# A second DMA queue for every other chunk of expert weights

## The chip, the core and the metric

The kernel runs on one core of a Trainium2 chip. The engines named below are TensorE (PE, matmuls), VectorE (DVE), ScalarE (ACT), GpSimd (POOL) and SyncE (SP), which here only asks for transfers and waits. Transfers from device memory (HBM) into the core's working memory are carried by 16 DMA engines; they are asked for in queues, which the profile numbers (q1 is the queue of SyncE, q10 that of ScalarE, q0 that of GpSimd). The metric is the device time of one execution in microseconds. Three executions of the kernel before took 1761.07, 1762.66 and 1762.74 us, a median of 1762.66.

## The reference

One layer of a diffusion backbone over 384 tokens (128 context tokens, 256 latent ones) of 1024 channels, in float32: a mixer (differential attention beside a two-directional state-space scan), then a mixture of 16 experts in which each expert chooses its tokens. Only the second half matters here:

```
def expert_choice_ffn(h, w_router, w_gate, w_up, w_down):
    xf = h.reshape(ntok, d)
    aff = jax.nn.softmax((xf @ w_router).astype(jnp.float32), axis=-1)
    gates, idx = lax.top_k(aff.T, cap)          # cap = 2 * tokens / 16: 16 context, 32 latent tokens
    xe = xf[idx]
    he = silu(einsum('ecd,edf->ecf', xe, w_gate)) * einsum('ecd,edf->ecf', xe, w_up)
    ye = einsum('ecf,efd->ecd', he, w_down) * gates[..., None]
    out = zeros_like(xf).at[idx.reshape(-1)].add(ye.reshape(-1, d))
```

Each expert has w_gate and w_up of 1024 x 2048 and w_down of 2048 x 1024, 24 MB in float32, so 384 MB for the 16 experts, and each weight is used once.

## The kernel before

The mixer comes first and takes a little under half of the time. The experts' weights are laid out ahead as 12 chunks an expert (`EC`), 192 in all, which I number n = 12 e + c for expert e and chunk c. A chunk is one transfer of 2 MB: 128 partitions, 16 KB each. Chunks c = 0 to 7 are alternately gate and up weights (c even: gate, c odd: up), four pairs j = 0 to 3. Chunks 8 to 11 are the down weights, two for each half of the output.

TensorE takes the chunks strictly in order, 32 matmuls a chunk (line 1002). After a gate and up pair ScalarE computes a Silu of the gate half (line 1483), VectorE multiplies the up half to it (line 2131), and TensorE later turns the product round (line 959) for the down chunks, which start only when the fourth product is turned. After chunks 9 and 11 ScalarE copies the result out (line 1491). After chunks 10 and 11 of every fourth expert TensorE combines the results of the four into the token rows (`combine`, lines 944 and 946). In the first four experts TensorE also has other pieces of work between chunks, lines 902 to 922.

The chunks lie in six slots (`FF_SLOTS`), and each slot has a semaphore of its own that its transfer raises by 16 when it has landed. Chunks 6, 7 and 8 of the first expert lie elsewhere, in early buffers. Chunk n + 6 may be asked for when chunk n has been used, since they share a slot; chunk 15 comes into the slot of chunk 9. What tells that a chunk is used is `ff_used` for an even c, `gu_ready` for c = 1, 3, 5, 7, and `d_ready0` and `d_ready1` for c = 9 and 11.

SyncE asks for all chunks, in the order of their use, in its one queue: `wait_used` waits for the slot, `load` asks (line 1039). Chunks 9 to 23 are written out one by one, the rest stand in a loop over experts 2 to 15. ScalarE, VectorE and TensorE run the experts in four groups of four: the first, a loop of two rounds for the middle two, and the last.

Of the kernel before, what the change touches and what calls it, by code (L numbers as in the profile page):

```python
# [33 lines left out]
NE, CAP_P, CAP_S, D_FF = 16, 16, 32, 2048  # L34
CAP = CAP_P + CAP_S
HALF = P // 2
GE = 4
# [6 lines left out]
FF_SLOTS = 6  # L44
# [34 lines left out]
EC = 12  # L79
# [86 lines left out]
def build(nc, t_in, t_out, consts, scratch):  # L166
    ctx = ExitStack()
    with ctx:
# [4 lines left out]
        def sem(name):  # L173
            if name not in sems:
                sems[name] = ctx.enter_context(nc.semaphore(name))
            return sems[name]

        def at(kib, *shape):

            n = int(np.prod(shape))  # L180
            off = int(kib * 256)
            assert off + n <= 53184, (kib, shape)
            v = arena[:, off:off + n]
            if len(shape) == 1:
                return v
            names = "abcd"[:len(shape)]
            return v.rearrange(f"p ({' '.join(names)}) -> p {' '.join(names)}",
                               **{k: s for k, s in zip(names[1:], shape[1:])})


        slots = [at(16 * s, KT, CW) for s in range(FF_SLOTS)]
# [112 lines left out]
        mixer_w, expert_w, dt_cols = t_in["mixer_chunks"], t_in["expert_chunks"], t_in["dt_columns"]  # L304
# [32 lines left out]
        pieces += [("xe_s", k) for k in range(KT)] + [("xe_p", n) for n in range(KT // 2)] + [("gate", n) for n in range(4)]  # L337
        beside_experts = {(n // 6, n % 6): p for n, p in enumerate(pieces) if p}
        piece_no = {p: n for n, (_, p) in enumerate(sorted(beside_experts.items()))}

        def y_sq(t, half):
            n = {0: 44, 1: 28, 2: 30}[t] + half
            return stat[:, n:n + 1]

        def of_group(g, r, per, add):

            return per * g + add if r is None else r * per + (per + add)
# [674 lines left out]
        @block.sync  # L1022
        def _(sp):
            sp.dma_start(vecs, t_in["vectors"]).then_inc(sem("vec_in"), 16)
            sp.dma_start(x_cm.rearrange("p k n -> p (k n)"), t_in["x_cm"]).then_inc(sem("x_in"), 16)
            def used(*key):
                name, value = AT["chunk_end"][chunk_no[key]]
                sp.wait_ge(sem(name), value)

            for n in range(NM - 2):  # L1030
                slot, m = chunk_slot[n], last_in_slot[n]
                if slot in (2, 3) and m is None:
                    sp.wait_ge(sem("ssd_over"), 1)
                if m is not None:
                    name, value = AT["chunk_end"][m]
                    sp.wait_ge(sem(name), value)
                sp.dma_start(weight_slot[slot].rearrange("p k n -> p (k n)"), mixer_w[n]).then_inc(sem(f"w_in_slot{slot}"), 16)
            def load(e, c, s):
                sp.dma_start(slots[s].rearrange("p k n -> p (k n)"), expert_w[e, c]).then_inc(sem(f"ff_slot{s}"), 16)

            def load_early(c, dst, k0):
                n_ = dst.shape[1]
                sp.dma_start(dst.rearrange("p k n -> p (k n)"), expert_w[0, c, :, k0 * CW:(k0 + n_) * CW])\
                  .then_inc(sem(f"ff_early{c}"), 16)

            def wait_used(e, c):

                if c >= 8 and c % 2:
                    sp.wait_ge(sem(f"d_ready{(c - 8) // 2}"), e + 1)
                elif c % 2:  # L1050
                    sp.wait_ge(sem("gu_ready"), e * 4 + (c // 2 + 1))
                else:
                    sp.wait_ge(sem("ff_used"), e * 6 + (c // 2 + 1))

            used("ga", 1)
            load(0, 0, 2)
            used("ada", 9)
            load(0, 1, 3)
            sp.wait_ge(sem("attn_over"), 1)
            for n in (NM - 2, NM - 1):  # L1060
                slot = chunk_slot[n]
                sp.dma_start(weight_slot[slot].rearrange("p k n -> p (k n)"), mixer_w[n]).then_inc(sem(f"w_in_slot{slot}"), 16)
            load(0, 3, 5)
            used("out", 0)
            load(0, 4, 0)
            used("out", 1)
            load(0, 5, 1)
            load_early(7, early_7a, 0)
            load_early(7, early_7b, 6)
            used("ada", 10)  # L1070
            load_early(6, early_6, 0)
            sp.wait_ge(sem("yg_ready"), 6)
            load_early(8, early_8a, 0)
            used("ada", 11)
            load(0, 2, 4)
            sp.wait_ge(sem("x_free"), AT["routed"])
            load_early(8, early_8b, 4)
            for n in range(9, 24):
                m = n - 9 if n < 15 else n - 6
                wait_used(m // 12, m % 12)  # L1080
                load(n // 12, n % 12, (n + 5) % FF_SLOTS)
            with sp.Fori(2, NE) as e:
                for c in range(12):
                    wait_used(e - 1 if c < 6 else e, (c - 6) % 12)
                    load(e, c, (c + 5) % FF_SLOTS)
            for n, t in enumerate(TILES):
                sp.wait_ge(sem("out_ready"), n + 1)
                dst = t_out["xs"][0, (t - 1) * P:t * P, :] if t else t_out["xp"][0]
                sp.dma_start(dst, x[:, t, :]).then_inc(sem("x_stored"), 16)
            sp.wait_ge(sem("x_stored"), 16 * NT)  # L1090
# [100 lines left out]
        def _(act):  # L1191
# [266 lines left out]
            def diagonals(n):  # L1458
                if n >= 2:
                    act.wait_ge(sem("piece_ready"), piece_no["gate", n - 2] + 1)  # L1460
                cnd, j = n // 2, n % 2
                for q in range(4):
                    act.activation(diag[:, n % 2, q, :], ident, ACT.Copy,
                                   scale=gpost[:, KT + 4 * j + q, cnd:cnd + 1]).then_inc(sem("diag2_ready"), 1)

            for j in range(2):
                act.activation(route[:, 4 + j:5 + j], stat[:, 32 + j:33 + j], ACT.Copy).then_inc(sem(f"d_free{j}"), 1)

            def group(g, r=None):

                first, final = g == 0, g == NE // GE - 1

                def N(per, add):
                    return of_group(g, r, per, add)

                for i in range(GE):
                    if first and i == 1:
                        diagonals(0)
                        diagonals(1)
                    for j in range(4):  # L1480
                        act.wait_ge(sem("gu_ready"), N(16, 4 * i + j + 1))
                        act.wait_ge(sem("h_done"), N(16, 4 * i + j + 1))
                        act.activation(sg[:, j % 2, :], psum[:, j % 2, 0:2 * P], ACT.Silu).then_inc(sem("sg_ready"), 1)  # L1483
                        if first and i == GE - 1 and j < 2:
                            diagonals(2 + j)
                    for j in range(2):
                        act.wait_ge(sem(f"d_ready{j}"), N(GE, i + 1))
                        for q in range(1 if final and i == GE - 1 and j else 2):
                            c0 = j * CW + q * 2 * P
                            for dst, lo in ((stage_s, 0), (stage_p, CAP_S)):  # L1490
                                cp = act.activation(dst[CAP_S * i:CAP_S * (i + 1), c0:c0 + 2 * P],  # L1491
                                                    psum[HALF * q + lo:HALF * q + lo + CAP_S, 5 + j, 0:2 * P], ACT.Copy)
                        cp.then_inc(sem(f"d_free{j}"), 1)
                        if final and i == GE - 1:
                            for n, t in enumerate(TILES):
                                act.wait_ge(sem("comb_done"), N(6, 3 * j + n + 1))
                                act.activation(last_sq[:, j, t, :], y[:, t, j * CW:(j + 1) * CW], ACT.Square, scale=D ** -0.5,
                                               accum_out=y_sq(t, j)).then_inc(sem("last_sq_ready"), 1)

            group(0)  # L1500
            with act.Fori(0, NE // GE - 2) as r:
                group(None, r)
            group(NE // GE - 1)


        @block.vector
# [706 lines left out]
```

## Time and profile before

| | |
|---|---|
| median of three executions | 1762.66 us |
| the profiled execution | 1757.46 us, of which its span 1755.7 us |
| TensorE busy | 1546.1 us, 88% of the span |
| VectorE / ScalarE busy | 475.7 us / 326.0 us |
| moved by DMA | 512.91 MB, 489.89 MB of it in SyncE's queue |
| DMA rate, second half of the span | 423 to 428 GB/s in each slice but the last |

The page cuts the span in 40 slices of 43.9 us and gives for each the busy share of the engines and of the 16 DMA engines, and the GB/s that they moved. A share of idle time matters only on the path that sets the end; the chain of waits names that path. In the table of DMA issues "to landing" is the time from the instruction that asks to the last byte landed, with what stands ahead of it in the queue. A matmul that is held up by a transfer is listed as waiting for "DMA arena<-in_expert_chunks".

### The profile page before, as it was taken

What the parts mean: (1) busy time and instruction counts of PE and PEld (TensorE: products, weight loads), DVE (VectorE), ACT (ScalarE), POOL (GpSimd) and SP (SyncE); (2) the same over time, 40 slices, a digit from 0 to 9 for tenths busy, and PEclk for the clock granted to TensorE, in tenths of its full rate; (3) what the DMA queues carried; (4) which work ended last, traced back from release to release, by engine and by line L of the source; (5) the groups of instructions that cost most, each with busy time, mean ns of one, the idle gap of its engine ahead of it and who ended that gap; (6) DMA issues with size and microseconds to landing.
All of it is one profiled execution on the core that took longest, in us unless ns stands there. A gap on an engine that the chain in (4) does not pass through costs nothing.

```text
span 1755.7 us, 22492 instructions
## 1 busy us (share of the span) xinstructions
PE 1546.1 (88%) x9269; PEld 917.5 (52%) x9269; DVE 475.7 (27%) x1181; ACT 326.0 (19%) x897; POOL 88.4 (5%) x116
## 2 busy tenths in 40 slices
PE   6999999999999999999999888777888787877776
PEld 4655555565545555556666455444455454544443
DVE  2336778740015555325111110000100000100003
ACT  1327565610012222012100100000000000000001
POOL 0002222200000001000000000000000000000000
PEclk9999999999999999999999999999999999999999
DMA  8234344224331523369999999999999999999995
GB/s 350 96 111 168 120 151 137 91 90 185 126 108 48 192 96 117 125 287 386 372 428 427 428 426 427 428 427 428 426 423 427 426 428 427 428 427 427 428 428 216
DMA packets 40593, 512.91 MB, mean 292 GB/s; under 512 B 4640, under 2 KB 4768, under 8 KB 10544
## 3 DMA queue, kind: packets, MB, share of 16 engines
q1 hardware_dynamic: 34416, 489.89, 67.2%
q0 software_dynamic: 5936, 21.01, 3.5%
q8 instruction: 77, 1.26, 0.3%
q10 hardware_dynamic: 144, 0.59, 0.1%
q14 instruction: 20, 0.16, 0.0%
HBM read 506.65 MB, written 4.82 MB: 291 GB/s over the span
## 4 chain that ended last, share of the span: by engine, by line
PE 55%; DMA 32%; DVE 7%; ACT 4%; issue 2%; SPq 0%; DVEq 0%; POOL 0%; ACTq 0%
DMA arena<-in_expert_chunks 32%; PE psum L1002 17%; PE psum L656 7%; PE psum L411 6%; PE psum L422 5%; PE psum L628 5%; PE psum L712 2%; PE psum L820 2%; PE psum L434 1%; ACT arena L1320 1%; ACT arena L1308 1%; PE psum L463 1%; PE psum L704 1%; DVE arena L1725 1%; PE psum L944 1%
## 5 line engine op out<-in xcount | busy, mean ns | idle before, releaser
L1002 PE MATMUL psum<-arena 128*64 128x256 f32 x6144 | 705.6, 385 | 139.8 <-DMA arena<-in_expert_chunks 107.9
L1002 PEld LDWEIGHTS psum<-arena 128*64 128x64 f32 x6144 | 437.6, 138 | 401.4 <-DMA arena<-in_expert_chunks 152.3
L2131 DVE TENSOR_TENSOR arena<-arena,psum 128x256 f32<-128x256 f32 x64 | 27.0, 421 | 703.3 <-ACT arena L1483 703.3
L411 PE MATMUL psum<-arena 128*128 128x384 f32 x512 | 168.9, 487 | 2.8 <-ACT arena L1227 2.8
L411 PEld LDWEIGHTS psum<-arena 128*128 128x128 f32 x512 | 96.2, 190 | 68.6 <-issue 3.3
L656 PE MATMUL psum<-arena 128*128 128x384 f32 x384 | 129.6, 491 | 0.0
L1483 ACT ACTIVATE arena<-psum 128x256 f32<-128x256 f32 x64 | 24.6, 384 | 564.8 <-PE psum L1002 564.8
L422 PE MATMUL psum<-arena 128*128 128x512 f32 x288 | 127.9, 600 | 0.0
L1491 ACT ACTIVATE arena<-psum 32x256 f32<-32x256 f32 x126 | 47.3, 375 | 274.5 <-PE psum L1002 273.4
L656 PEld LDWEIGHTS psum<-arena 128*128 128x128 f32 x384 | 72.5, 193 | 46.9 <-issue 3.2
L1105 POOL TENSOR_TENSOR arena<-arena 128x1 f32<-128x1 f32 x45 | 25.9, 577 | 1332.0 <-DVE arena L2172 941.6
L422 PEld LDWEIGHTS psum<-arena 128*128 128x128 f32 x288 | 55.7, 195 | 68.7 <-issue 67.9
L628 PE MATMUL psum<-arena 128*128 128x384 f32 x256 | 83.3, 487 | 1.8 <-DVE arena L1702 1.2
L628 PEld LDWEIGHTS psum<-arena 128*128 128x128 f32 x256 | 48.5, 190 | 36.3 <-DVE arena L1702 1.5
L1308 ACT ACTIVATE arena<-arena 128x128 f32<-128x128 f32 x192 | 57.2, 386 | 0.0
L712 PE MATMUL psum<-arena 128*128 128x384 f32 x128 | 42.1, 487 | 2.1 <-DVE arena L1849 1.7
L820 PE MATMUL psum<-arena 128*128 128x512 f32 x96 | 42.5, 595 | 0.0
L959 PE MATMUL psum<-arena 128*128 128x128 f32 x128 | 27.5, 297 | 13.0 <-DVE arena L2097 12.9
L463 PE MATMUL psum<-arena 128*128 128x128 f32 (+1 forms) x215 | 36.3, 279 | 1.7 <-DVE arena L1940 1.7
L1384 ACT ACTIVATE arena<-psum,arena 128x384 f32<-128x384 f32 (+1 forms) x48 | 24.0, 506 | 65.4 <-DVE arena L1827 65.4
L463 PEld LDWEIGHTS psum<-arena 128*128 128x128 f32 (+1 forms) x215 | 25.3, 140 | 20.2 <-issue 14.6
L712 PEld LDWEIGHTS psum<-arena 128*128 128x128 f32 x128 | 24.1, 190 | 19.2 <-issue 2.4
(274 smaller groups left out, 1130.4 us busy)
## 6 DMA issues: line engine op xcount, KB each, us to landing
arena<-in_expert_chunks SPq DMA_DIRECT2D x190, 2048.0 KB, 25.4
arena<-in_mixer_chunks SPq DMA_DIRECT2D x40, 2048.0 KB, 8.5
arena<-cs_rows POOLq DMA_DIRECT2D x24, 512.0 KB, 5.1
arena<-in_h_cm POOLq DMA_DIRECT2D x8, 256.0 KB, 3.2
out_state<-arena POOLq DMA_DIRECT2D x8, 256.0 KB, 2.6
arena<-in_expert_chunks SPq DMA_DIRECT2D x2, 1024.0 KB, 15.9
arena<-in_x_cm SPq DMA_DIRECT2D x1, 1536.0 KB, 8.7
arena<-in_expert_chunks SPq DMA_DIRECT2D x1, 1536.0 KB, 11.1
```

Source lines behind the costliest of these rows:

```text
L411: mm = pe.matmul(b[:, 0:NTOK], w[:, k, ct * P:(ct + 1) * P], src[:, k, :], start=k == 0, stop=k == KT - 1)
L422: mm = pe.matmul(b[:, :], h1T[:, k, t * P:(t + 1) * P], w[:, k, :], start=k == 0, stop=k == KT - 1)
L463: mm = pe.transpose(b[0:width, at_:at_ + rows], src, ident[0:rows, 0:rows])
L628: mm = pe.matmul(psum[:, (n0 + ct) % 4, 0:NTOK], w[:, k, ct * P:(ct + 1) * P], oT[:, k2 * KT + k, :], start=k2 == 0 and k == 0, stop=k2 == ...
L656: mm = pe.matmul(b[:, 0:NTOK], w[:, k, n % 4 * P:(n % 4 + 1) * P], h1T[:, k, :], start=k == 0, stop=k == KT - 1)
L712: mm = pe.matmul(psum[:, o_bank[ct], 0:NTOK], w[:, k, ct % 4 * P:(ct % 4 + 1) * P], oTa[:, k, :], start=k == 0, stop=k == KT - 1)
L820: mm = pe.matmul(b[:, :], mergedT[:, k, t * P:(t + 1) * P], w_o[:, k, :], start=k == 0, stop=k == KT - 1)
L959: mm = pe.transpose(psum[:, 4, a * P:(a + 1) * P], h_sb[:, j % 2, a * P:(a + 1) * P], ident)
L1002: mm = pe.matmul(psum[HALF * q:HALF * (q + 1), bank, 0:2 * P], src[:, k0 + k, :], w_k[:, 2 * P * q:2 * P * (q + 1)], start=bool(opens and ...
L1308: last = act.activation(e_, e_, ACT.Identity, scale=-1.0, bias=cs[:, t, 32 * d + 8 * g + h:32 * d + 8 * g + h + 1])
L1491: cp = act.activation(dst[CAP_S * i:CAP_S * (i + 1), c0:c0 + 2 * P], psum[HALF * q + lo:HALF * q + lo + CAP_S, 5 + j, 0:2 * P], ACT.Copy)
L2131: dve.tensor_tensor(h_sb[:, j % 2, :], sg[:, j % 2, :], psum[:, 2 + j % 2, 0:2 * P], ALU.mult)\
```

## The change

From chunk 15, the sixteenth, on, SyncE asks only for chunks of even number. ScalarE asks for those of odd number, in its own queue: for chunk n + 6 right after its wait for the gate and up pair that ends in chunk n (before the Silu), or right after its wait for the down half that ends in chunk n (before the copies). Slots, semaphores and the condition for each chunk are as before. The loop of ScalarE over the two middle groups is written out, since the chunk numbers are now needed while the program is built.

```
             for n in range(9, 24):
                 m = n - 9 if n < 15 else n - 6
-                wait_used(m // 12, m % 12)
-                load(n // 12, n % 12, (n + 5) % FF_SLOTS)
+                if m < 6 or n % 2 == 0:
+                    wait_used(m // 12, m % 12)
+                    load(n // 12, n % 12, (n + 5) % FF_SLOTS)
             with sp.Fori(2, NE) as e:
-                for c in range(12):
+                for c in range(0, 12, 2):
                     wait_used(e - 1 if c < 6 else e, (c - 6) % 12)
                     load(e, c, (c + 5) % FF_SLOTS)
...
+            def load_six_on(e, c):
+
+                n = EC * e + c + FF_SLOTS
+                if 15 <= n < NE * EC:
+                    sl = (n + 5) % FF_SLOTS
+                    act.dma_start(slots[sl].rearrange("p k n -> p (k n)"), expert_w[n // EC, n % EC])\
+                       .then_inc(sem(f"ff_slot{sl}"), 16)
+
...
                     for j in range(4):
                         act.wait_ge(sem("gu_ready"), N(16, 4 * i + j + 1))
+                        load_six_on(GE * g + i, 2 * j + 1)
                         act.wait_ge(sem("h_done"), N(16, 4 * i + j + 1))
...
                     for j in range(2):
                         act.wait_ge(sem(f"d_ready{j}"), N(GE, i + 1))
+                        load_six_on(GE * g + i, 9 + 2 * j)
...
-            group(0)
-            with act.Fori(0, NE // GE - 2) as r:
-                group(None, r)
-            group(NE // GE - 1)
+            for g in range(NE // GE):
+                group(g)
```

SyncE's loop over experts 2 to 15, its first half, before. A row is an instruction with what it waits for; the DMA rows each ask for one chunk, the rows between compute the number to wait for.

```order
L1039 ISA [waits ff_used]
L1039 DMA arena<-in_expert_chunks 128x4096
L1051 ISA
L1039 ISA [waits gu_ready]
L1039 DMA arena<-in_expert_chunks 128x4096
L1053 REGISTER_ALU
L1039 ISA [waits ff_used]
L1039 DMA arena<-in_expert_chunks 128x4096
L1039 ISA [waits d_ready0]
L1039 DMA arena<-in_expert_chunks 128x4096
```

The same place in SyncE's loop after the change.

```order
L1039 ISA [waits ff_used]
L1039 DMA arena<-in_expert_chunks 128x4096
L1053 REGISTER_ALU
L1039 ISA [waits ff_used]
L1039 DMA arena<-in_expert_chunks 128x4096
L1053 REGISTER_ALU
```

Of four chunks asked for in one queue two are left, and both wait for `ff_used`; the ones behind `gu_ready` and `d_ready0` are gone from it.

ScalarE in the first expert, from its last Silu on, and the start of the second expert, before. Line 1483 is the Silu, line 1491 the copies of a down half, line 1463 a piece of other work.

```order
L1483 ACTIVATE arena<-psum 128x256 [waits h_done,gu_ready] x3
L1491 ACTIVATE arena<-psum 32x256 [waits d_ready0]
L1491 ACTIVATE arena<-psum 32x256 x3
L1491 ACTIVATE arena<-psum 32x256 [waits d_ready1]
L1491 ACTIVATE arena<-psum 32x256 x3
L1463 ACTIVATE arena<-arena 128x128 x8
L1483 ACTIVATE arena<-psum 128x256 [waits h_done,gu_ready] x4
```

The same place after. Line 1472 asks for a chunk; the Silu is now line 1493, the copies line 1502, the other work line 1464.

```order
L1493 ACTIVATE arena<-psum 128x256 [waits h_done,gu_ready] x3
L1472 DMA arena<-in_expert_chunks 128x4096 [waits d_ready0]
L1502 ACTIVATE arena<-psum 32x256 x4
L1472 DMA arena<-in_expert_chunks 128x4096 [waits d_ready1]
L1502 ACTIVATE arena<-psum 32x256 x4
L1464 ACTIVATE arena<-arena 128x128 x8
L1472 DMA arena<-in_expert_chunks 128x4096 [waits gu_ready]
L1493 ACTIVATE arena<-psum 128x256 [waits h_done]
```

The first transfer that moves to ScalarE is chunk 15, behind `d_ready0` of the first expert; from then on each of the six waits of an expert has one behind it, ahead of the arithmetic.

## Rows read from the trace of the kernel before

**Rows 1.** The page: DMA busy tenths and GB/s in 40 equal slices.

```profile
DMA  8234344224331523369999999999999999999995
GB/s 350 96 111 168 120 151 137 91 90 185 126 108 48 192 96 117 125 287 386 372 428 427 428 426 427 428 427 428 426 423 427 426 428 427 428 427 427 428 428 216
```

**Rows 2.** Stretches: length, busy us (x instructions) by engine, PEclk, DMA share, GB/s.

```profile
855.00:857.00 2.00, 2.00 (x20) 1.22 (x16) 0.00 (x0) 0.34 (x1) 0.00 (x0) 1.00 0.00 0
...
870.00:1700.00 830.00, 682.48 (x5662) 415.00 (x5658) 72.10 (x171) 66.46 (x177) 0.00 (x0) 0.99 1.01 427
...
1285.00:1295.00 10.00, 10.00 (x91) 6.35 (x89) 0.53 (x2) 0.77 (x2) 0.00 (x0) 1.00 0.99 411
```

**Rows 3.** Waits, 870 to 1735 us: us in total, times, longest.

```profile
PEld psum L1002 <- DMA arena<-in_expert_chunks: 152.3, 105, 2.8
```

**Rows 4.** The chain that ended last: start us, us, what.

```profile
1616.88 25.48 DMA arena<-in_expert_chunks
1646.25 25.48 DMA arena<-in_expert_chunks
```

**Rows 5.** TensorE's last four chunks: start us, us, line [idle before <- releaser].

```profile
1719.85 0.20 PEld L959 LDWEIGHTS psum<-arena 128*128 128x128 f32 x2 [0.38 <-issue]
...
1722.21 3.67 PE L1002 MATMUL psum<-arena 128*64 128x256 f32 x32 [0.52 <-DVE arena L2097]
...
1731.98 3.67 PE L1002 MATMUL psum<-arena 128*64 128x256 f32 x32 [1.04 <-DMA arena<-in_expert_chunks]
1735.59 0.30 PEld L944 LDWEIGHTS psum<-arena 128*128 128x128 f32 x2 [0.39 <-issue]
...
1738.36 3.67 PE L1002 MATMUL psum<-arena 128*64 128x256 f32 x32
```

**Rows 6.** Stretches while the last chunks land.

```profile
1725.00:1726.00 1.00, 0.89 (x10) 0.29 (x5) 0.00 (x0) 0.00 (x0) 0.00 (x0) 1.00 1.03 426
1726.00:1727.00 1.00, 0.00 (x0) 0.00 (x0) 0.00 (x0) 0.00 (x0) 0.00 (x0) 1.00 0.57 229
...
1732.00:1734.00 2.00, 2.00 (x20) 1.35 (x22) 0.00 (x0) 0.51 (x2) 0.00 (x0) 1.00 0.50 213
...
1736.00:1738.00 2.00, 2.00 (x6) 0.76 (x4) 1.08 (x2) 0.53 (x1) 0.00 (x0) 1.00 0.00 0
```

**Rows 7.** DMA queues, stretch 2 to 5 us: packets, MB, share.

```profile
q10 hardware_dynamic: 144, 0.59, 49.2%
q1 hardware_dynamic: 146, 0.41, 36.9%
```

**Rows 8.** TensorE, ScalarE and SyncE around chunks 10 to 15, and TensorE one expert later.

```profile
856.66 48.19 SPq L1039 DMA_DIRECT2D arena<-in_expert_chunks  x12
856.66 1.54 ACT L1491 ACTIVATE arena<-psum 32x256 f32<-32x256 f32 x4 [9.03 <-PE psum L1002]
...
864.78 7.13 PE L1002 MATMUL psum<-arena 128*64 128x256 f32 x64
...
873.32 7.13 PE L1002 MATMUL psum<-arena 128*64 128x256 f32 x64
```

**Rows 9.** What asking costs: duration ns min/median/max; then issue to landing.

```profile
L1039 SPq DMA_DIRECT2D arena<-in_expert_chunks x189: 327/333/462, 748.9 to 1710.3; - x189
...
DMA to landing us min/median/max: 7.5/25.4/28.8
```

**Rows 10.** The one DMA that ScalarE asks for, by its line.

```profile
L1210 ACTq DMA_DIRECT2D arena<-shape_consts x1: 412/412/412, 0.7 to 0.7; - x1
```

**Rows 11.** TensorE where its loop over the middle groups turns back.

```profile
1262.52 3.67 PE L1002 MATMUL psum<-arena 128*64 128x256 f32 x32
...
1269.65 1.02 PE L946 MATMUL psum<-arena 128*128 128x512 f32 x2
1274.40 0.86 PE L1002 MATMUL psum<-arena 128*64 128x256 f32 x5 [3.73 <-issue]
1279.53 14.91 PE L1002 MATMUL psum<-arena 128*64 128x256 f32 x123 [4.27 <-issue]
```

## The prediction

> **What bounds the kernel now.** I read the page's slices first. From slice 21 to slice 39 the DMA engines are busy all the time and the rate hardly moves, 423 to 428 GB/s [rows 1]. The stretch 870 to 1700 us says the same in one row: 427 GB/s at a share of 1.01, with TensorE busy 682 of 830 us [rows 2]. Then the waits: in the experts TensorE's weight loads are held up 105 times by expert chunks, 152.3 us in all [rows 3]. Last the chain of waits: near the end it is one transfer after another, 25.48 us each, and the pieces stand 1646.25 - 1616.88 = 29.37 us apart for six chunks, 4.895 us a chunk [rows 4], against 3.67 us of matmuls [rows 5]. So from about 865 us on the end is: the time at which the last byte has landed, plus what TensorE still has to do then. The change can move three things: the rate, the order in which chunks land, and idle time of the DMA engines.
>
> **How the last chunks run.** The last expert's chunk 10 (n = 190) starts at 1731.98, held up by its transfer; chunk 11 (n = 191) starts at 1738.36, and not for want of data: it follows the combine, 1738.36 - 1735.59 = 2.8 us [rows 5]. By the pace chunk 191 lands at 1731.94 + 4.9 = 1736.8; the DMA engines are at rest from 1736 on [rows 6]. I call the landing of the last byte T and take 1736 to 1736.8. Behind the start of chunk 191 nothing depends on a transfer, so the end moves as that start moves. The last chunk thus has about 2 us of slack today, and chunk 190 has none.
>
> **Part 1: the asking moves.** 89 chunks (n = 15, 17, ..., 191) go from SyncE to ScalarE. An issue takes SyncE 0.333 us [rows 9]; the only one of ScalarE took 0.412 us [rows 10]. So ScalarE gets 89 x 0.33 to 0.41 = 30 to 37 us more work, in front of Silus and copies, in a stretch of 900 us where it is busy 66 of 830 us [rows 2]. Behind the issue on ScalarE's queue stand the Silu, then VectorE's product, then TensorE's turn; but only the fourth Silu of an expert is waited for at once, and there the gap between the third turn and chunk 8 is 1722.21 - 1719.85 = 2.4 us [rows 5] and would grow by 0.33 to 0.41. What hides this is the DMA-bound pace: TensorE has 4.9 - 3.7 = 1.2 us of room a chunk. In the last expert, where the gap could count, its fourth wait has no chunk behind it (n would be 193). Cost 0; with the cover gone 15 x 0.33 to 15 x 0.41 = 5 to 6 us. SyncE loses the same issues and half its register work; it is not on the path: gain 0. Is ScalarE late for a slot? The slots of odd chunks come free exactly at its own waits, and it had idled 9.03 us when chunk 9 was used, at 856.66, the same moment at which SyncE asked for chunk 15 [rows 8]. Cost 0, at most some tenths of a microsecond at the one place where it matters: the DMA engines are at rest at 855 to 857 us and wait for this issue [rows 2]. Below zero there is nothing to gain, since the slot isn't free earlier.
>
> The written out loop: ScalarE's program is longer and doesn't turn back. TensorE and VectorE still do. Where TensorE turns back it stands idle 3.73 and 4.27 us [rows 11], and no slot comes free between the end of a chunk at 1262.52 + 3.67 = 1266.2 and that of the next, some 3 us after 1279.53 [rows 11]; six slots cover it nearly, the rate falls to 411 GB/s for 10 us [rows 2], worth 0.4 us. No effect of the change there as long as some four chunks stay queued. Value 0, bounds -1 and +3 (the upper one if only three chunks, 14.7 us, are queued there, as in the second rival below).
>
> **Part 2: two queues share the engines.** Before, chunk n has all 16 engines and n + 1 stands behind it. After, both are under way at once. Does the trace show sharing? Only once: at 2 to 5 us ScalarE's queue has 144 packets served and SyncE's 146, both with work left [rows 7]. Packet for packet, equal turns. A chunk is 128 equal rows of 16 KB whatever its number, so each queue gets half: a chunk takes 9.8 us instead of 4.9, and two are under way. No data are lost: T stays if the rate stays, since about five chunks are asked for at any time (25.4 us to landing [rows 9]) and neither queue runs dry.
>
> What changes is the order at the end. When chunk 190 lands, part of 191 is left, which then runs at full rate. If 191 follows at a distance d in the shared pace, 190 lands d/2 before T, where it landed 4.9 us before. The distance is set when the queues fill, at 865 to 900 us: TensorE frees the slot of an even chunk 3.57 us before that of the odd one (7.13 / 2), and the next even one 8.54 - 3.57 = 4.97 us later [rows 8]. So the queues start almost in alternation, d between 3.6 and 4.9, and as turns are equal it stays. I take 4.3: chunk 190 lands 2.15 us before T, at 1733.9 to 1734.7 instead of 1731.94: 2.0 to 2.7 us later, I take 2.3. The rest follows unchanged: 3.67, combine, chunk 191, the tail. Bounds of the tail without drift: d = 4.9 gives +1.6 (T = 1736), and both landing together (d = 0) gives +4.9.
>
> In the Trainium skill, "DMA: Bandwidth & Descriptors", section "Queues, rings and completion order", each DMA engine takes turns between queues packet by packet; the row above agrees. By that rule alone the sum is +2.3. The section "Issuing engines are not separate DMA queues" says that issuing from a second engine saves only the time to ask; by it there is no gain in rate here, which no row shows or excludes.
>
> **Part 3: the rate.** No row shows two queues with long transfers over a long time, so I bound it. Upward: at 1726 the rate falls from 426 to 229 GB/s, and stays near 213 until 1734 [rows 6]: half of the engines were done 8 us before the other half. Each engine has the same bytes, so the slow half is 8 of 870 us, 0.9%, slower. If two queues brought it to the pace of the fast half, T would come 8 us earlier. Downward: the worst stretch of 10 us in the rows has 411 GB/s [rows 2]; that over 870 us would be 870 x (427/411 - 1) = 34 us, but there it was missing slots. The row nearest to the case is the long one, 427 GB/s, with hardly any variation, and I take 0, with ends -8 and +34, of which I hold more than +8 (1%) unlikely.
>
> **Sum.** 0 + 0 + 2.3 + 0 = +2.3 us. The profiled execution took 1757.46 us (span 1755.7), so 1759.8 for it. The median of the timed ones is 5.2 us above the profiled one; I carry the difference over: 1762.66 + 2.3 = 1765.0 us.
>
> **Rivals.**
> A: two queues fill gaps between transfers. For: the slow half of the engines has 0.9% to gain. Against: share 1.01 in the long stretch leaves no gap to see. Then -8 + 2.3 = -5.7: 1757.0 us.
> In the same page of the Trainium skill, section "Where 436 GB/s comes from", the ceiling is 435 GB/s; by it the most to gain would be 1.9% of 870 us, some 16 us, an estimate from that page.
> B, the slower side: turns aren't equal, or the distance drifts, and one queue runs ahead until the slots stop it. It decides as soon as one queue gets 1% more: 4 us more in 400 us. Then the late queue has the engines alone at the end, one chunk per 4.9 us, each followed by one that has long landed. If the odd queue is ahead, 188 lands at T - 4.9, about 1731.9, and 188, 189 and 190 follow, 11.0 us, then 2.8 of combining: 191 starts at 1745.7 instead of 1738.36, +7.4. If the even queue is ahead, 187 lands at about 1727.0; four chunks 14.7, the gap 2.4, combining 2.8: 1746.9, +8.5. For: half the engines are already 0.9% off the other half. Against: the equal packets of rows 7. 1770 to 1771 us.
> C: alternating between queues costs rate, 1% or more. For: nothing in the trace. Against: the 427 GB/s don't suffer from the small packets of other queues. +8.7 + 2.3 = +11: 1773.7 us.
> D: ScalarE's issues aren't hidden, or an issue stalls its engine while the queues are full. Against: SyncE's issues take 0.333 us with five chunks queued, at most 0.462 [rows 9]. +5 to +6 on top: 1771 us.
>
> **Chances.** Forecast 0.43 (own range +0.5 to +5, 1763 to 1768); A 0.2; B 0.2; C 0.1; D 0.07. What a measurement can tell from no change is 0.2%, 3.5 us. Faster: A, 0.2. Same: about four fifths of the forecast's case and a little of A's, 0.37. Slower: the rest of the forecast's case, B, C and D, 0.43. The range takes in A and B and leaves out half of C: 1756 to 1772.
>
> **What would show it.** Queue q10 with 89 transfers of 2 MB and q1 with the others; to-landing times near 25 us in both. A rate of 427 GB/s in the middle, else A or C. Landings alternate with some 4 and 5 us between them: TensorE's waits for data then stay single; if it waits before every second chunk only, for twice as long, that is B. The last two chunks within 2 to 3 us of each other, chunk 190 starting 2 to 3 us later against T. A gap before chunk 8 that is 0.3 to 0.4 us longer, without effect. Wrong it would be if the long stretch's rate is off by over 0.3%, or if chunk 190 starts at the old distance from T.

## The result

The change made the kernel slower by little: the ratio to before is 1.0023, with a 95% interval of 1.0015 to 1.0032, or about 4 us (2.6 to 5.6). The medians of 20 executions each are 1763.95 us (1760.9 to 1768.4) after and 1761.05 us (1757.7 to 1763.8) before, 2.9 us apart. The forecast was 1765.0 us, which is +2.3 on a base of 1762.66 from three executions.

The profiled execution of after has a span of 1761.7 us, 6.0 more than that of before. The page's slices and its table of queues:

```profile
DMA  8234334224321423279999999999999999999994
GB/s 349 96 110 167 120 135 152 94 86 190 120 107 49 191 96 136 105 292 401 374 428 427 427 426 427 427 427 427 427 384 427 427 427 427 426 428 427 427 427 202
```

```profile
arena<-in_expert_chunks SPq DMA_DIRECT2D x101, 2048.0 KB, 25.0
arena<-in_expert_chunks ACTq DMA_DIRECT2D x89, 2048.0 KB, 25.6
```

Against [rows 1] the rate is the same to 2 GB/s from the 21st slice on, but for the last one, in which the transfers end (202 for 216), and one near 1290 us: 384 where 423 stood. The two queues split the chunks as meant, and their times to landing are those of [rows 9]. Three stretches of after (length, busy us by engine, PEclk, DMA share, GB/s):

```profile
870.00:1700.00 830.00, 690.23 (x5630) 420.91 (x5626) 71.81 (x171) 66.33 (x177) 0.00 (x0) 0.97 1.00 425
1285.00:1295.00 10.00, 10.00 (x74) 6.03 (x72) 0.37 (x1) 0.38 (x1) 0.00 (x0) 0.77 0.66 242
1738.00:1739.00 1.00, 1.00 (x8) 0.55 (x6) 0.00 (x0) 0.00 (x0) 0.00 (x0) 0.50 0.00 0
```

In the long stretch of [rows 2] 2 GB/s are missing, and the second row has them: for 10 us the rate is 242 GB/s, 43% under the 427 of elsewhere, where before had 411 GB/s. The third row is chunk 190: TensorE's granted clock is 0.50, its lower level of 1.2 GHz. TensorE's last chunks in after, to be held against [rows 5] (start us, us, line, what ended the idle time before):

```profile
1724.03 0.44 PE L959 MATMUL psum<-arena 128*128 128x128 f32 x2
...
1726.60 7.30 PE L1002 MATMUL psum<-arena 128*64 128x256 f32 x64 [0.72 <-DVE arena L2106]
...
1736.30 5.36 PE L1002 MATMUL psum<-arena 128*64 128x256 f32 x32 [2.41 <-DMA arena<-in_expert_chunks]
1741.59 1.98 PE L944 MATMUL psum<-arena 128*128 128x512 f32 x4
...
1743.41 1.02 PE L946 MATMUL psum<-arena 128*128 128x512 f32 x2
...
1744.37 3.67 PE L1002 MATMUL psum<-arena 128*64 128x256 f32 x32
```

And the DMA engines while the last bytes land, against [rows 6]:

```profile
1736.50:1737.00 0.50, 0.50 (x6) 0.34 (x4) 0.00 (x0) 0.00 (x0) 0.00 (x0) 0.76 0.39 164
1737.00:1737.50 0.50, 0.50 (x6) 0.30 (x4) 0.00 (x0) 0.00 (x0) 0.00 (x0) 0.50 0.08 33
```

I read from these rates that the last byte is moved at about 1737.3, and chunk 190 starts 1.0 us ahead of that. Before, it started 3.9 us ahead (1731.98 against about 1735.9). That is 2.9 us, the order of landing. Chunk 190 then takes 5.36 us instead of 3.67: 1.7 us. And the last byte itself comes later.

The rows of the last two requests say the same more sharply, since the time of asking and the time to landing add up to the landing. First chunk 190, asked for by SyncE, then chunk 191, asked for by ScalarE:

```profile
L1039 SPq DMA_DIRECT2D arena<-in_expert_chunks x1: 333/333/333, 1710.8 to 1710.8; - x1
DMA to landing us min/median/max: 25.4/25.4/25.4
...
L1472 ACTq DMA_DIRECT2D arena<-in_expert_chunks x1: 335/335/335, 1714.4 to 1714.4; - x1
DMA to landing us min/median/max: 23.7/23.7/23.7
```

Chunk 190 lands at 1736.3 (the chain of waits has it as 1710.82 + 25.44), when TensorE starts on it, and chunk 191 at 1738.1, 1.8 us behind. In before the same two rows give 1705.3 + 26.7 = 1732.0 and 1710.3 + 26.5 = 1736.8, one chunk's 4.9 us apart. So the order of landing is worth about 3 us. A landing is reported about 1 us after the rate has gone to zero, in before as in after.

To compare single executions I count from the start of the experts' first chunk, since what comes ahead of it varies by up to 5 us from one execution to the next, in kernels that are the same up to there. That chunk starts at 816.49 in before and 816.97 in after:

```profile
816.49 7.13 PE L1002 MATMUL psum<-arena 128*64 128x256 f32 x64 [0.92 <-DVE arena L2045]
```

```profile
816.97 7.13 PE L1002 MATMUL psum<-arena 128*64 128x256 f32 x64 [0.92 <-DVE arena L2054]
```

From there to the start of chunk 191 it is 921.9 us before and 927.4 after, +5.5 us. The sum: the last byte 919.4 to 920.3 us after the start, +0.9; the order +2.9; the clock +1.7. Behind the start of chunk 191 both kernels are alike (17.3 us to the end of the span). The 5.5 us of this pair of profiles lie at the upper end of what the executions give, 2.6 to 5.6 us by the ratio; the section on the prediction comes back to that.

### The profile page after: what moved, and what is told of

The parts are those of the page before. It is cut to its first block, busy times and chain, and to the rows that moved or that the text cites. A ratio compares the mean times of both kernels' runs of the same rounds, so it can differ in the third digit from the quotient of the medians.

```text
span 1761.7 us, 22164 instructions
## 1 busy us (share of the span) xinstructions
PE 1559.6 (89%) x9269; PEld 926.8 (53%) x9269; DVE 478.2 (27%) x1181; ACT 325.8 (18%) x897; POOL 88.0 (5%) x116
## 4 chain that ended last, share of the span: by engine, by line
PE 54%; DMA 34%; DVE 6%; ACT 3%; issue 2%; ACTq 0%; DVEq 0%; SPq 0%; POOL 0%
DMA arena<-in_expert_chunks 33%; PE psum L1002 16%; PE psum L656 7%; PE psum L411 6%; PE psum L422 6%; PE psum L628 5%; PE psum L712 2%; PE psum L820 2%; PE psum L434 1%; ACT arena L1309 1%; ACT arena L1321 1%; PE psum L944 1%; PE psum L463 1%; PE psum L704 1%; PE psum L610 1%
## 5 line engine op out<-in xcount | busy, mean ns | idle before, releaser
L1002 PE MATMUL psum<-arena 128*64 128x256 f32 x6144 | 716.8, 390 | 126.0 <-DMA arena<-in_expert_chunks 89.3
L1002 PEld LDWEIGHTS psum<-arena 128*64 128x64 f32 x6144 | 446.6, 140 | 390.5 <-DMA arena<-in_expert_chunks 127.8
L411 PEld LDWEIGHTS psum<-arena 128*128 128x128 f32 x512 | 96.2, 190 | 68.6 <-issue 3.3
L656 PEld LDWEIGHTS psum<-arena 128*128 128x128 f32 x384 | 72.5, 193 | 46.9 <-issue 3.2
L422 PEld LDWEIGHTS psum<-arena 128*128 128x128 f32 x288 | 55.9, 195 | 69.1 <-issue 68.3
L628 PEld LDWEIGHTS psum<-arena 128*128 128x128 f32 x256 | 48.5, 190 | 36.3 <-DVE arena L1711 1.5
L959 PEld LDWEIGHTS psum<-arena 128*128 128x128 f32 x128 | 12.9, 140 | 40.8 <-DVE arena L2140 22.4
## 6 DMA issues: line engine op xcount, KB each, us to landing
arena<-in_expert_chunks ACTq DMA_DIRECT2D x89, 2048.0 KB, 25.6
```

The costliest lines, as they stand in the source:

```text
L411: mm = pe.matmul(b[:, 0:NTOK], w[:, k, ct * P:(ct + 1) * P], src[:, k, :], start=k == 0, stop=k == KT - 1)
L422: mm = pe.matmul(b[:, :], h1T[:, k, t * P:(t + 1) * P], w[:, k, :], start=k == 0, stop=k == KT - 1)
L628: mm = pe.matmul(psum[:, (n0 + ct) % 4, 0:NTOK], w[:, k, ct * P:(ct + 1) * P], oT[:, k2 * KT + k, :], start=k2 == 0 and k == 0, stop=k2 == ...
L656: mm = pe.matmul(b[:, 0:NTOK], w[:, k, n % 4 * P:(n % 4 + 1) * P], h1T[:, k, :], start=k == 0, stop=k == KT - 1)
L959: mm = pe.transpose(psum[:, 4, a * P:(a + 1) * P], h_sb[:, j % 2, a * P:(a + 1) * P], ident)
L1002: mm = pe.matmul(psum[HALF * q:HALF * (q + 1), bank, 0:2 * P], src[:, k0 + k, :], w_k[:, 2 * P * q:2 * P * (q + 1)], start=bool(opens and ...
```

## The experiments

The table gives for each kernel the ratio to before with its interval, and from its profile the time from the start of the experts to the last byte (T) and to the start of chunk 191. T is read from the rate, good to half a microsecond only. The last column is how far chunk 190 lands ahead of chunk 191, from the rows of their requests as above, good to 0.1 us.

| kernel | ratio (95%) | to T | to chunk 191 | 190 ahead of 191 |
|---|---|---|---|---|
| before | 1 | 919.4 | 921.9 | 4.9 |
| the change | 1.0023 (1.0015 to 1.0032) | 920.3 | 927.4 | 1.8 |
| e1, only the written out loop | 0.9997 (0.9988 to 1.0006) | 918.8 | 921.7 | 4.9 |
| e2, last expert in one queue | 0.9998 (0.9989 to 1.0007) | 920.2 | 922.6 | 4.9 |
| e3, one queue, last two swapped | 1.0042 (1.0028 to 1.0056) | 919.0 | 927.9 | -4.9 |
| e4, change, TensorE written out | 1.0010 (1.0001 to 1.0019) | 917.5 | 922.7 | 1.8 |
| e5, before, TensorE written out | 0.9992 (0.9981 to 1.0002) | 918.2 | 920.7 | 4.9 |
| e6, e4 with last expert in one queue | 0.9992 (0.9983 to 1.0000) | 917.3 | 919.9 | 4.9 |
| e7, change, long filler | 1.0033 (1.0021 to 1.0045) | 920.6 | 928.2 | 1.6 |
| e8, e5 with chunk 190 in halves | 0.9986 (0.9978 to 0.9995) | 917.5 | 918.6 | 4.8 (its first half 7.3) |
| e9, change, short filler | 1.0021 (1.0012 to 1.0030) | 919.4 | 925.0 | 1.8 |
| e10, change, chunk 191 by SyncE | 1.0004 (0.9996 to 1.0013) | 919.9 | 922.8 | 4.9 |

**e1: the written out loop of ScalarE alone.**

```
-            group(0)
-            with act.Fori(0, NE // GE - 2) as r:
-                group(None, r)
-            group(NE // GE - 1)
+            for g in range(NE // GE):
+                group(g)
```

> Only ScalarE's loop is written out; SyncE asks for every chunk in its one queue, as before. Theory 1 (the order in which the last chunks land costs the time): no change, within 0.1% of before; chunk 190 starts some 4 us ahead of the last byte. Rival (the longer program of ScalarE, or what it fetches, costs the time): +3 us, like the whole change.

Measured 0.9997. The longer program costs nothing that can be seen; the queues are what matters.

**e2: two queues, but the last expert's chunks all by SyncE.**

```
-            with sp.Fori(2, NE) as e:
+            with sp.Fori(2, NE - 1) as e:
...
+            for c in range(12):
+                wait_used(NE - 2 if c < 6 else NE - 1, (c - 6) % 12)
+                load(NE - 1, c, (c + 5) % FF_SLOTS)
...
-                if 15 <= n < NE * EC:
+                if 15 <= n < (NE - 1) * EC:
```

> Two queues as in the change up to chunk 179; the last expert's twelve chunks (180 to 191) are all asked for by SyncE, in order. Theory 1: chunk 190 again lands one chunk's time (4.9 us) before 191, the end comes 3 to 4.5 us earlier than with the change, so equal to before within 0.1%, unless engines were idle in the middle. Rival (the rate, or an idle spell of the DMA engines in the middle, costs the time): nothing is won, still +3 us against before.

Measured 0.9998, the interval (0.9989 to 1.0007) below that of the change. Its profile has the same hole in the transfers as after (246 GB/s from 1285 to 1295 us), and T as late; but chunk 190 starts about 4 us ahead of T, at full clock:

```profile
1733.28 3.67 PE L1002 MATMUL psum<-arena 128*64 128x256 f32 x32 [1.41 <-DMA arena<-in_expert_chunks]
1736.88 1.98 PE L944 MATMUL psum<-arena 128*128 128x512 f32 x4
1738.70 1.02 PE L946 MATMUL psum<-arena 128*128 128x512 f32 x2
1739.65 3.67 PE L1002 MATMUL psum<-arena 128*64 128x256 f32 x32
```

So the loss sits in the last dozen chunks, not in the 83 that ScalarE asks for before.

**e3: the late chunk 190 without a second queue.**

```
+            wait_used(NE - 1, 5)
+            load(NE - 1, 11, (11 + 5) % FF_SLOTS)
+            load(NE - 1, 10, (10 + 5) % FF_SLOTS)
```

(in place of the last two loads in the order 10, 11).

> One queue as before, but SyncE asks for chunk 191 ahead of chunk 190 (it waits for the slot of 191 first). The cost of a late chunk 190 by itself, with no second queue: it lands with the last byte, 4.9 us later against it. Theory 1: +4 to +5 us against before from the order, and +1.7 us more if TensorE's clock falls to half in chunk 190 after the longer wait, so +5 to +7 us (0.3 to 0.4%). Rival (landing order doesn't matter, since chunk 191 has slack): 0 to +2 us.

Measured 1.0042 (+7 us, 5 to 10). The whole 4.9 us of a chunk are paid, and the clock on top (4.99 us instead of 3.67; the granted clock is 0.50 from 1738 to 1741 us):

```profile
1739.55 4.99 PE L1002 MATMUL psum<-arena 128*64 128x256 f32 x32 [6.75 <-DMA arena<-in_expert_chunks]
```

The order of landing costs what it says, in one queue as in two. The rival, that chunk 191's slack covers it, is out.

**e5: TensorE's loop written out, one queue.** The diff is that of e1 with `pe` for `act`.

> One queue as before; TensorE's loop over the two middle groups is written out, so that it doesn't turn back. If turning back alone made TensorE stand still (3.73 and 4.27 us) and the DMA rate dip (411 GB/s at 1285 us), both go, and the time falls by at most 1 us: the dip was worth 0.4 us. If it is program fetch behind the transfers of weights, in whatever form the program has, gaps of the same size stay, and the longer program could add new ones: up to +5 us.

Measured 0.9992, the interval just reaching 1. Where TensorE stood still before [rows 11] it now goes on 1.05 us after the combine. Elsewhere in the experts its longest idle time that no other engine and no transfer accounts for is 2.5 us:

```profile
1274.73 1.02 PE L946 MATMUL psum<-arena 128*128 128x512 f32 x2
1276.80 14.03 PE L1002 MATMUL psum<-arena 128*64 128x256 f32 x128 [1.05 <-DVE arena L2118]
```

So the standing still comes with the turning back; the same instructions, written out, have none of it. What TensorE does in that time no row shows.

**e4: the change, TensorE's loop written out.**

> The change, with TensorE's loop over the middle groups written out. Theory 1 with its second half (the queues keep their distance until an idle spell of the DMA engines resets it; that spell comes from TensorE turning back): no stretch at 242 GB/s near 1290 us, so the last byte lands 1 to 1.4 us earlier against the start of the experts; TensorE waits some 1.2 us before every chunk to the end instead of 2.1 us before every second; chunk 190 lands 2.4 instead of 2.0 us ahead of the last byte. +0.5 to +2.5 us against before. Rival (the distance drifts by itself, turns are unequal): pairs come back, +3 to +5 us as with the change.

Measured 1.0010, inside what theory 1 gave. The hole is gone, and T is 2.8 us earlier, more than the 1 to 1.4 expected. The chunks stay apart to the end: TensorE waits before each one, 0.6 and 1.5 us in turn, where after has 7.34 us of two chunks and then 2.1 us of waiting.

```profile
1285.00:1295.00 10.00, 10.00 (x92) 6.44 (x90) 0.76 (x2) 0.38 (x1) 0.00 (x0) 1.00 1.00 424
```

```profile
1708.51 3.67 PE L1002 MATMUL psum<-arena 128*64 128x256 f32 x32 [0.59 <-DMA arena<-in_expert_chunks]
...
1714.03 3.67 PE L1002 MATMUL psum<-arena 128*64 128x256 f32 x32 [1.48 <-DMA arena<-in_expert_chunks]
...
1733.60 3.67 PE L1002 MATMUL psum<-arena 128*64 128x256 f32 x32 [1.86 <-DMA arena<-in_expert_chunks]
```

A pair in after, for comparison:

```profile
1706.97 7.34 PE L1002 MATMUL psum<-arena 128*64 128x256 f32 x64 [2.07 <-DMA arena<-in_expert_chunks]
```

One part was expected wrongly: chunk 190 does not land 2.4 us ahead of chunk 191 but 1.8, as in after (1708.1 + 25.5 = 1733.6 and 1712.2 + 23.2 = 1735.4), though there was no idle spell. So the idle spell is not what brings the last two together. Against e5, the same kernel with one queue, the order costs about 3 us (4.9 - 1.8), T is 0.7 earlier, and chunk 191 starts 2.0 us later, 0.11%. By the two ratios it is 0.18%; their intervals, 0.1% to either side, hold both.

**e6: both mended.** Two queues to chunk 179, the last expert by SyncE, TensorE written out.

> Two queues up to chunk 179, the last expert by SyncE alone, TensorE's loop written out. It stands to the kernel with one queue and TensorE written out (0.9992 of before) as two queues in the middle stand to one, with neither the idle spell nor the late chunk 190. Theory 1: the same as that kernel, 0.999 of before. Rival (two queues cost or gain rate in the middle): off by 0.2% or more either way; a gain of the slow half of the DMA engines would show as up to 8 us.

Measured 0.9992, the same as e5. Two queues in the middle neither win nor lose, to the 0.15% (2.6 us) that two such intervals can tell apart: this also excludes the 8 us that the slow half of the DMA engines might have won.

**e7: matmuls in front of chunk 190.**

```
+                        if final and i == GE - 1 and c == 10:
+                            for _ in range(5):
+                                pe.matmul(psum[:, 7, :], ident, hT.rearrange("p k s -> p (k s)")[:, 0:CW], start=True, stop=True)
```

> The change, with five matmuls more (some 2.5 us, their result is not used) on TensorE ahead of its wait for chunk 190. If the clock falls in chunk 190 because TensorE stood still ahead of it, chunk 190 takes 3.67 us instead of 5.36 and the end comes 1.7 us earlier, +1 to +2.5 us against before. Rival (the clock falls for what TensorE did over a longer time): no gain, +3 us or a little more.

Measured 1.0033: the filler was mis-sized. It took 4.56 us, not 2.5, and ended when chunk 190 had landed for some time. But chunk 190 itself ran at full clock:

```profile
1736.68 4.56 PE L974 MATMUL psum<-arena 128*128 128x512 f32 x10
1741.17 3.67 PE L1005 MATMUL psum<-arena 128*64 128x256 f32 x32
```

**e9: the same with two matmuls** (`range(2)`).

> As the kernel with five matmuls ahead of chunk 190, but with two. The five took 4.56 us and ran past the landing of chunk 190; two take 1.8 us of a wait of 2.4 us. If standing still ahead of chunk 190 is what drops the clock in it, chunk 190 takes 3.67 us and nothing is delayed: +1.7 us less than the change, so +1 to +2.5 us against before. Rival (the clock follows a longer stretch, the waits of 2.1 us before every second chunk among it): chunk 190 still takes over 5 us, +3 to +4 us.

In the profile it does what was expected: the filler fits in the wait, chunk 190 takes 3.67 us, and chunk 191 starts 2.4 us earlier than in the change (925.0 against 927.4).

```profile
1734.41 1.99 PE L974 MATMUL psum<-arena 128*128 128x512 f32 x4
1737.15 3.67 PE L1005 MATMUL psum<-arena 128*64 128x256 f32 x32 [0.75 <-DMA arena<-in_expert_chunks]
```

The times don't bear it out: 1.0021, against 1.0023 of the change, where I expected 1.0006 to 1.0014. The intervals are too wide to tell 1.7 us apart, and one profile doesn't show in how many executions of the change the clock falls. Nor are the two profiles with a filler a proof that it keeps the clock up. In after, of 14 waits of 2.0 to 2.7 us for a transfer between 880 and 1716 us, 10 were followed by chunks at full clock, 4 by a pair like this one:

```profile
1658.05 8.81 PE L1002 MATMUL psum<-arena 128*64 128x256 f32 x64 [2.06 <-DMA arena<-in_expert_chunks]
```

So chunk 190 could have run at full clock in e7 and e9 by chance. That the clock fell in chunk 190 of after, and what it cost there, is measured; that the wait just ahead of it is the cause, and that 1.7 us stand in the median, is not shown.

**e10: one issue moved back.**

```
+            wait_used(NE - 1, 5)
+            load(NE - 1, 11, (11 + 5) % FF_SLOTS)
...
-                if 15 <= n < NE * EC:
+                if 15 <= n < NE * EC - 1:
```

> The change, with one issue moved back: chunk 191 is asked for by SyncE, behind 190; 88 odd chunks stay with ScalarE. Theory 1: chunk 190 shares the DMA engines only with what is left of 189 and then has them alone, 191 follows, so 190 again lands 4.9 us ahead of the last byte and chunk 190 runs at full clock: the 4.7 us of the tail are gone, and what is left against before is the idle spell's 1 us, 0 to +1.5 us. Rival (the cost stems from the 80 chunks before): +2.5 us or more stay.

Measured 1.0004 (0.9996 to 1.0013), clear of the change's 1.0015 to 1.0032. With chunk 191 behind 190 in one queue, and nothing else changed, chunk 190 had landed before TensorE came to it (chunks 188 to 190 run through, the middle row of three), although the pairs ahead of it are those of after:

```profile
1718.97 7.34 PE L1002 MATMUL psum<-arena 128*64 128x256 f32 x64 [2.07 <-DMA arena<-in_expert_chunks]
...
1728.80 10.75 PE L1002 MATMUL psum<-arena 128*64 128x256 f32 x96 [0.71 <-DVE arena L2108]
...
1742.25 3.67 PE L1002 MATMUL psum<-arena 128*64 128x256 f32 x32
```

**e8: a version that beats both.** One queue, TensorE written out, chunk 190 in two transfers of 1 MB.

```
+                if c == 10:
+                    for k0, name in ((0, "ff_slot3"), (4, "ff_last")):
+                        sp.dma_start(slots[3][:, k0:k0 + 4].rearrange("p k n -> p (k n)"),
+                                     expert_w[NE - 1, c, :, k0 * CW:(k0 + 4) * CW]).then_inc(sem(name), 16)
...
+                            if final and i == GE - 1 and c == 10 and k == 4:
+                                pe.wait_ge(sem("ff_last"), 16)
```

> One queue, TensorE written out, and chunk 190 asked for in two halves with a semaphore each, so that TensorE starts on the first half when it has landed. By theory 1 chunk 190's landing sets the end: TensorE is done with it half a chunk of matmuls (1.8 us) earlier, and chunk 191 starts 1.8 us earlier, if it has landed: 1.4 + 1.8 = 3.2 us faster than before, 0.998. Rival (chunk 191's landing sets the end): no more than the 1.4 us of the written out loop.

Measured 0.9986 (0.9978 to 0.9995), a median of 1757.69 us. TensorE runs through chunks 188 to 190 without a wait, and chunk 191 starts 918.6 us after the experts' start, 3.3 us earlier than before, for 3.2 expected:

```profile
1724.66 10.94 PE L1004 MATMUL psum<-arena 128*64 128x256 f32 x96 [0.52 <-DVE arena L2105]
...
1738.31 3.67 PE L1004 MATMUL psum<-arena 128*64 128x256 f32 x32
```

Chunk 191 lands at 1712.6 + 25.6 = 1738.2, and starts at 1738.31. So its slack of some 1.6 us before is used up, and cutting chunk 190 finer would win nothing more. The kernel is faster than before and after; that it beats e5 (by 2.1 us in the profiles) is within their intervals.

## Why the prediction was right, and where it wasn't

**The bound.** Right. The end is the last byte plus what TensorE has left; behind the start of chunk 191 nothing changed.

**Part 1, the asking.** Right in size: each of the 89 issues takes ScalarE 0.334 us, and with it the wait for ScalarE's copies before the second combine grows from 1.63 to 2.01 us (a row of before and one of after).

```profile
1267.83 1.98 PE L944 MATMUL psum<-arena 128*128 128x512 f32 x4 [1.63 <-ACT arena L1491]
```

```profile
1271.76 3.04 PE L944 MATMUL psum<-arena 128*128 128x512 f32 x4 [2.01 <-ACT arena L1502]
```

Hidden it is almost everywhere; e1 excludes the written out loop, and e6 shows that the 83 issues in the middle cost nothing measurable. The one place where such tenths come on the path is the next point.

**The idle spell.** Wrong: I gave 0, with a bound of +3 only if three chunks were queued. The step that failed is that no effect would come as long as the queues keep their distance. When two chunks share the engines in turns, each lands when half of its neighbour has landed as well, so half a chunk, 2.45 us, later against the bytes moved. I used that for chunk 190 and forgot it for the others. TensorE is later by as much all along: chunk 91, the eighth of expert 7, starts 425.0 us after the experts' start in before and 427.7 in after.

```profile
1241.51 3.67 PE L1002 MATMUL psum<-arena 128*64 128x256 f32 x32 [1.26 <-DMA arena<-in_expert_chunks]
```

```profile
1244.69 3.67 PE L1002 MATMUL psum<-arena 128*64 128x256 f32 x32 [1.23 <-DMA arena<-in_expert_chunks]
```

So its slots come free later and less is queued when TensorE turns back. There it stands still for 7.5 us, no longer than the 8.0 of [rows 11], but it comes there later: by those 2.7 us (3.1 by the first combine), by the 0.4 of ScalarE's issue and by a combine at a lower clock (3.04 and 1.71 us, the row above and the first below, for what takes 1.98 and 1.02 elsewhere), together 5.2 us. It restarts 4.7 us later against before:

```profile
1274.59 1.71 PE L946 MATMUL psum<-arena 128*128 128x512 f32 x2
...
1278.34 0.86 PE L1002 MATMUL psum<-arena 128*64 128x256 f32 x5 [2.04 <-issue]
1284.70 16.01 PE L1002 MATMUL psum<-arena 128*64 128x256 f32 x123 [5.50 <-issue]
```

What was 0.4 us of transfer time lost in 10 us, (1 - 411/427) x 10, is now (1 - 242/427) x 10 = 4.3 us. T moved by only 0.9 us, since half of the engines were ahead and could lose more: in after the halves end 4 to 5 us apart (full rate to 1732, more than half of it to 1734, the end at 1737), not 8 to 9 us as in [rows 6]. Against the start of the experts the first half ends over 5 us later than before and the second 0.9, on average some 3 of the 3.9 us that the spell cost more. With TensorE written out the spell is gone and T is 2.8 us earlier (e4 against the change). e1 and e3, with one queue, also dipped, to 378 and 365 GB/s; so the dip varies; but in after and in e2, e7, e9 and e10, the kernels with two queues and the loop, it is deeper each time, 234 to 269. That it is deeper for TensorE's coming later is my reading; no run moves that by itself.

**Part 2, the order.** Right in mechanism, and too small in size: 2.0 to 2.7 us were forecast, 2.3 taken, 2.9 measured, about 3 by the landings. From 1000 to 1700 us the two queues carried 148.21 and 148.28 MB.

```profile
q1 hardware_dynamic: 10174, 148.21, 49.9%
q10 hardware_dynamic: 10183, 148.28, 49.9%
```

The Trainium skill says in "DMA: Bandwidth & Descriptors", section "Queues, rings and completion order", that a DMA engine takes turns between the queues that it has work for, packet by packet; the trace agrees, with 10174 packets against 10183. Equal bytes alone would not prove it, since six slots that are used in strict order hold both queues to the same number of chunks. But a queue that got more turns would run ahead until the slots stop it, and its chunks would have landed long before they are used. In after TensorE waits for the chunks of both queues alike up to the idle spell, and near the end chunk 189 still lands 3.7 us behind chunk 188 (1704.6 + 25.6 = 1730.2 and 1701.0 + 25.5 = 1726.5).

What was mis-sized is the distance and the end. That the distance stays as it was at the start held only up to the idle spell: before it TensorE waits 1.23 us before each chunk (the row at 1244.69 above), after it two chunks run at a stretch. So d is 3.7 us, not 4.3, and half of it is the 1.8 us by which chunk 190 lands ahead of 191. And chunk 191 had landed at 1736.8 in before, the later end of what I took for T. With both, the sum of the prediction gives 4.9 - 1.8, about 3 us, what the landings show. It does not take the idle spell for this: e4, without it, has the same 1.8 us.

**Part 3, the rate.** Right where the queues were full: 427 GB/s in all slices but one, and e6 against e5 no difference. But a sign that I had named for being wrong did come: the long stretch has 425 GB/s for 427, 0.5% less, where 0.3% was the limit. It is the idle spell: 185 GB/s less for 10 us are 1.9 MB, and 2 GB/s less for 830 us are 1.7 MB. With the spell gone (e4, e6) the stretch has 427 again. Rival A (the slow half catches up) and rival C (alternating costs rate) are out.

**What the sum missed.** The sum supposed that chunk 190 takes 3.67 us, as before. After a wait of 2.41 us the granted clock was 0.50 from 1737 to 1740 us, and it took 5.36. Before had waited 1.04 us there [rows 5], and the clock stayed at 1. I had put this term at nothing without a reason.

**Rival B**, one queue far ahead with +7.4 or +8.5, did not come, although its sign did: from the idle spell on TensorE waits before every second chunk only, and for twice as long. The sign was badly chosen. Chunks 3.7 and 6.1 us apart show it as well, since TensorE takes 3.67 us for one; in B the second would have landed long before. **Rival D** did not come either: ScalarE's 89 issues took 334 to 335 ns each, with the queues full.

So the forecast of +2.3 us lies just under the interval of the measured +4 (2.6 to 5.6) and inside its own range of +0.5 to +5. The profiles put the difference into the order (some 0.6 us more) and the two terms that I had at zero, 0.9 us for the idle spell and up to 1.7 us for the clock. If the clock fell in chunk 190 as often as behind the other waits of that length, in 4 of 14, it would cost 0.5 us on average, and the sum would be 0.9 + 2.9 + 0.5 = 4.3 us; that is an estimate from one profile. That the medians, 2.9 us apart, come within 0.6 us of the forecast is in part luck, with a term of 0.9 us and one of up to 1.7 us left out. The base of 1762.66 was 1.6 us over the median of twenty executions, so 1765.0 is 1.05 us over the measured 1763.95.

## What to carry to other kernels

Two queues that share saturated DMA engines move no more bytes, but they change which transfer is done when: each lands about half a transfer later (2.7 us at chunk 91, with 4.9 us a transfer), and at the end the last two land 1.8 us apart instead of 4.9. Where one transfer is needed ahead of another, ask for both in one queue, at least for the last ones; one issue moved back was enough here (e10). And look at what the consumer waits for last: with that one transfer cut in two the last chunk started 2.1 us earlier (e8 against e5, in the profiles), where the second queue only delayed it.

## What the hardware showed that I had not expected

- TensorE's clock: in chunk 190 it fell to half (PEclk 0.50, 1.2 GHz) after 2.4 us of standing still in after and 6.75 us in e3, and stayed at full level after 1.0 us in before, 1.2 in e5 and 1.86 in e4. It was at full level too in e7 and e9, where matmuls filled the wait. The length of the wait alone doesn't decide: in after 10 of 14 waits of 2.0 to 2.7 us were followed by chunks at full clock (7.3 us a pair), 4 by pairs of 8.7 to 8.8. The mean over 870 to 1700 us is 0.97 in after, with its waits of 2.1 us before every second chunk, against 0.99 before.
- Of 16 DMA engines that carry the same bytes, half end some 8 us ahead of the others after 870 us, with one queue as in e1 and e5; where they had the long idle spell, as in after, it is 4 to 5 us.
- TensorE stands still for some 8 us, 3.73 and 4.27 us [rows 11], where its loop over the middle groups turns back while the DMA engines are saturated. Written out, the same instructions run through, and the kernel is not slower for its length (0.9992). Whether the saturated DMA engines have a part in it no run shows.
